# A two-model transformer kernel on one core: residue-order copies on GpSimd, maxima spread by transposes, and the cross attention rebuilt

## The chip, the cores and the metric

One core of a Trainium2 chip runs the whole program. The metric is the device time of one execution in microseconds (us), as a median over runs. A profiled execution gives the rows that are quoted here. In them PE is TensorE, PEld its weight loads, DVE is VectorE, ACT is ScalarE, POOL is GpSimd and SP is SyncE, whose queue issues all DMAs.

## The reference

A sequence of 512 tokens with 1024 channels passes through two blocks of two layers each, all in float32. The first block's layers have a dilated-window attention, a stick-breaking attention, gates and a convolutional feed-forward part. The second block's layers have a mixer (convolution and pooling in the first, mLSTM and latent attention in the second), a cross attention over 256 memory tokens, and a SwiGLU part.

```python
# first block, mixer A: query t attends keys t - j*dilation; three groups of heads
DSW_GROUPS = ((128, 1), (512, 4), (2048, 16))
def to_sub(a):
    a = a.reshape(B, L, dilation, H, hd).transpose(0, 2, 3, 1, 4)
...
# second block, in each layer after the mixer
def memory_cross_attention(h, mem_n, wq, wkv, wo):
    q = (h @ wq).reshape(B, S, XA_HEADS, XA_HEAD_DIM)          # 4 heads of 128
    k, v = jnp.split(mem_n @ wkv, 2, axis=-1)                   # 256 memory tokens
    ...
    s = jnp.einsum('bshd,bmhd->bhsm', q, k) * (XA_HEAD_DIM ** -0.5)
    p = jax.nn.softmax(s, axis=-1)
    return jnp.einsum('bhsm,bmhd->bshd', p, v).reshape(B, S, XA_WIDTH) @ wo

x = x + mix
mem_n = rmsnorm_2(mem, mem_norm_g[layer])
x = x + memory_cross_attention(rmsnorm_2(x, norm_xattn_g[layer]), mem_n, ...)
x = x + swiglu(rmsnorm_2(x, norm_ffn_g[layer]), ...)
```

## The kernel before

**Layout.** The activations `x` lie in SBUF with channels on partitions: 8 tiles (`KT`) of 128 channels by 512 tokens. Every projection is computed in three products of split operands: a value is split into a high part in fp32r and the remainder, `h_hi` and `h_lo` for activations, `w_hi` and `w_lo` for weights, and `product` (lines 607 to 609) issues high by high, high by low and low by high for each tile of the contraction. An operand that isn't split (scores, sums, values of an attention) goes through TensorE as plain float32; such a matmul leaves two records in the trace. A transpose against the identity leaves one.

**The weight stream.** The weights come in numbered chunks, in the order of `chunk_starts`: `qk`, `v`, `gate`, `br`, `wo`, `up`, `down` and so on. SP loads a chunk into `stage`, which holds one chunk in two parts; the load of a part waits until VectorE has taken the remainder of the same part of the chunk before (`w_lo_done`). ScalarE writes `w_hi` (line 1108) as soon as the chunk two places ahead of it has been used by TensorE (`w_used`), and VectorE writes `w_lo` from `stage` and `w_hi` (line 1503). So `w_hi` and `w_lo` hold two chunks. TensorE starts a chunk when its `w_lo` is done and the result banks `M` of the chunk two places before have been read (`m_free`). Each engine's order of work is written out by hand; an instruction that waits holds up everything behind it on its engine.

**First block.** `qk0` and `qk1` are 8 chunks each. The 4 chunks of values `v` follow (`token_major`): here activations are the stationary operand and 256 columns of weights the moving one. For the first and last chunk a stationary tile is 128 tokens in a row. For the two chunks between (groups 1 and 2), `residue_tile` picks every fourth token out of `h_hi` and `h_lo`, since these groups are attended in residue order. Then `mixture_head` runs 4 times a layer: scores, a part of the gate projections (`gate_tile`), the spread of the row maxima over partitions (line 747, a plain float32 matmul of a broadcast column with the identity, 12 for a head), more gate projection, 15 transposes of the probabilities (line 756), values. GpSimd does nothing.

**Cross attention, per layer (`cross_attention`).** Ahead of it stands the mixer's output product of 4 chunks: `ev_out` in the first layer, whose h tiles of the next norm are made while it runs, and `od_out` in the second, where `held=True` puts all 8 pairs of them behind its last chunk. Then TensorE does: the first chunk of q (`xq`), tile by tile as `h_lo` comes (`first_tiles`); the spread of the norm (line 666); 16 transposes of the memory, which VectorE copies to `mem_t`; the second chunk of q; 4 chunks of memory keys and values (`xkv`), with squares, sums and a norm of their own for the memory (`MEMORY`); and `attend`, a loop over 4 heads: scores of the next head, 8 transposes of the probabilities (line 931), a copy back by ScalarE (line 1357), the product with the values (line 937), and the split of the result into `xo_hi` and `xo_lo`. A head uses the four banks `A` or the four banks `M`. When all 4 heads are done, 4 chunks of `xo` (256 KB a part instead of 512) give the output product, and the feed-forward part starts with `first_tiles` over `up`.

Of the kernel before, what the change touches and what calls it, by code (L numbers as in the profile page):

```python
# [73 lines left out]
for _l in range(DEPTH):  # L74
    NORMS += [(KT if _l else 0, KT)] + ([(3, 3), (2, 2)] if _l else []) + [(KT, KT)] * 3
NORMS += [(KT, 0)]
LAST_NORM = len(NORMS) - 1
MIX, XATTN, MEMORY, FFN = ([5, 9], [6, 12], [7, 13], [8, 14])
LATENT_Q, LATENT_KV = 10, 11
# [58 lines left out]
def chunk_starts():  # L138
# [6 lines left out]
    for l in range(DEPTH):  # L145
# [5 lines left out]
        sizes += [(f"xq{l}", 2), (f"xkv{l}", 4), (f"xo{l}", 4)]  # L151
# [9 lines left out]
def block_program(nc, dram, out):  # L161
# [12 lines left out]
    with ExitStack() as ctx:  # L174
# [64 lines left out]
        def lay(*items):  # L239
# [17 lines left out]
        mem_t, mem_hi, mem_lo, k_x, v_x, q_x, x_prob, x_turned, mem_tok = lay(  # L257
            (8, "mem_t", [KT, N_MEM], F32),
# [71 lines left out]
        mem_turned, mem_out = sem("mem_turned"), sem("mem_out")  # L330
# [14 lines left out]
        chain = sem("chain")  # L345
        branch_done, value_done, col_root, col_done = (
# [17 lines left out]
        def head_banks(h):  # L364
            return A if h % 2 == 0 else M

# [15 lines left out]
        def gain_at(n, k):  # L382

            if n == MIX[0]:
# [3 lines left out]
                           MEMORY[0]: ("mem_norm_g_2", 0), MEMORY[1]: ("mem_norm_g_2", KT),  # L388
# [34 lines left out]
        def columns_before(n):  # L423

            return sum(j < n for j in (*WITH_COLUMNS, *MEMORY))
# [9 lines left out]
        def _(sp):  # L435
# [93 lines left out]
            def cross_attention(l):  # L529
                for n in range(2):  # L530
                    load_tiles(start[f"xq{l}"][0] + n, by_tile(dram["xattn_wq_2"][l]), 2 * n)
# [4 lines left out]
                for n in range(2):  # L536
                    load_wide(c0 + 2 + n, w, 2 + n)
                for n in range(4):
# [49 lines left out]
            for n in range(4):  # L588
                load_tiles(start["od_out"][0] + n, by_tile(dram["od_w_out_2"][0]), 2 * n)
                if n == 2:  # L590
# [10 lines left out]
        def _(pe):  # L601
# [38 lines left out]
            def token_major(c, s, hi, lo, k, tiles, pick=None):  # L640

                chunk_in(c)
                for t in range(tiles):
                    def tokens(n):
                        if pick is None:
                            return hi[:, n, t * P:(t + 1) * P], lo[:, n, t * P:(t + 1) * P]
                        return pick(hi[:, n, :], t), pick(lo[:, n, :], t)
# [8 lines left out]
            def norm(n, tokens=S):  # L656

                pe.wait_ge(square_added, additions(n + 1))
                if n in WITH_COLUMNS or n in MEMORY:
# [67 lines left out]
            def mixture_head(l, h):  # L727
# [115 lines left out]
            for l in range(DEPTH):  # L843
# [4 lines left out]
                for g in range(GROUPS):  # L848
                    def residue_tile(t, n, g=g):

# [1359 lines left out]
```

## Time and profile before

| | |
|---|---|
| median of 3 runs | 3119.66 us (3118.12 to 3121.15) |
| the profiled execution | 3118.83 us; its span, first to last instruction, 3116.7 us |
| instructions in it | 35330 |
| TensorE busy | 2946.1 us, 95% |
| VectorE, ScalarE, GpSimd busy | 1615.0, 1122.1 and 0.2 us |
| mean granted TensorE clock | 0.971 |
| HBM read | 247.86 MB, 80 GB/s over the span |

The profile page gives the busy time of each engine, the granted clock in 40 slices, the chain of work that ended last, and the costliest groups of instructions. Other views of the same trace give stretches (busy time, clock), waits (who waited for whom), the chain in order of time, and the instructions in order of time. Matmuls overlap in the pipeline, so their durations can't be added up; the distance between starts is what one costs in a run of them.

### The profile page before, as it was taken

How to read it: one execution, taken by the hardware profiler on the slowest of the kernel's cores; microseconds unless marked ns; L12 is line 12 of the kernel's file. 1: busy time of each engine (PE TensorE's matmuls, PEld its weight loads, DVE VectorE, ACT ScalarE, POOL GpSimd, SP SyncE). 2: the span in 40 equal slices, each digit the busy share in tenths (PEclk: the TensorE clock that was granted, in tenths of full speed). 3: DMA queues.
4: the chain of work that ended last, by engine and by line, in shares of the span. 5: the costliest groups of instructions: out<-in, count | busy, mean ns of one | idle time of the engine just before them, and what ended most of it. 6: DMA issues, size and time to landing. Idle time of an engine off the chain costs nothing.

```text
span 3116.7 us, 35330 instructions
## 1 busy us (share of the span) xinstructions
PE 2946.1 (95%) x13434; PEld 2398.0 (77%) x13434; DVE 1615.0 (52%) x2249; ACT 1122.1 (36%) x1544; POOL 0.2 (0%) x4
## 2 busy tenths in 40 slices
PE   5999989999999998999999989999996879899998
PEld 4898778888889877888888768888883547688886
DVE  3347656545534765644676554435443555454344
ACT  2116535324312653432442443223333243343222
POOL 0000000000000000000000000000000000000000
PEclk9999999999999999999999989999997889999999
DMA  3311123332331112333243223332320202133322
GB/s 116 95 41 55 55 81 94 90 100 87 101 95 41 55 54 81 101 91 105 83 123 95 88 62 100 87 108 82 108 74 4 58 21 68 57 106 94 108 84 78
DMA packets 465250, 251.37 MB, mean 81 GB/s; under 512 B 14982, under 2 KB 461279, under 8 KB 465023
## 3 DMA queue, kind: packets, MB, share of 16 engines
q1 hardware_dynamic: 465151, 250.00, 27.6%
q8 instruction: 69, 1.13, 0.1%
q14 instruction: 30, 0.25, 0.0%
HBM read 247.86 MB, written 2.10 MB: 80 GB/s over the span
## 4 chain that ended last, share of the span: by engine, by line
PE 88%; DVE 5%; ACT 3%; DMA 1%; issue 1%; SPq 0%; DVEq 0%; ACTq 0%
PE M L607 24%; PE M L609 24%; PE M L608 24%; PE M L682 2%; PE M L683 2%; PE M L684 2%; DVE w_lo L1503 1%; PE A L803 1%; PE A L739 1%; PE A L771 1%; PE A L937 1%; PE M L937 1%; PE A L747 1%; ACT w_hi L1108 1%; PE A L815 1%
## 5 line engine op out<-in xcount | busy, mean ns | idle before, releaser
L607 PE MATMUL M<-h_hi,w_hi 128*128 128x512 f32 (+1 forms) x2272 | 894.5, 394 | 1.7 <-DVE h_lo L1937 1.7
L609 PE MATMUL M<-h_hi,w_lo 128*128 128x512 f32 (+1 forms) x2272 | 886.2, 390 | 0.0
L608 PE MATMUL M<-h_lo,w_hi 128*128 128x512 f32 (+1 forms) x2272 | 886.1, 390 | 0.0
L1108 ACT ACTIVATE w_hi<-stage 128x1024 fp32r<-128x1024 f32 (+4 forms) x524 | 508.9, 1013 | 840.0 <-PE M L609 754.8
L1503 DVE TENSOR_TENSOR w_lo<-stage,w_hi 128x1024 fp32r<-128x1024 f32 (+4 forms) x524 | 595.6, 1174 | 133.9 <-ACT w_hi L1108 132.7
L607 PEld LDWEIGHTS M<-h_hi,w_hi 128*128 128x128 f32 (+1 forms) x2272 | 427.5, 188 | 94.7 <-issue 5.8
L608 PEld LDWEIGHTS M<-h_lo,w_hi 128*128 128x128 f32 (+1 forms) x2272 | 427.5, 188 | 90.7 <-issue 2.6
L609 PEld LDWEIGHTS M<-h_hi,w_lo 128*128 128x128 f32 (+1 forms) x2272 | 427.2, 188 | 90.2
L607 PE MATMUL M<-hid_hi,w_hi 128*128 128x512 f32 x704 | 274.6, 390 | 6.9 <-DVE hid_lo L1623 6.9
L608 PE MATMUL M<-hid_lo,w_hi 128*128 128x512 f32 x704 | 274.0, 389 | 0.0
L609 PE MATMUL M<-hid_hi,w_lo 128*128 128x512 f32 x704 | 273.9, 389 | 0.0
L1603 DVE TENSOR_TENSOR normed<-M,rstd 128x512 f32<-128x512 f32 x88 | 60.9, 692 | 313.7 <-PE M L609 282.0
L607 PEld LDWEIGHTS M<-hid_hi,w_hi 128*128 128x128 f32 x704 | 132.1, 188 | 36.7 <-DVE hid_lo L1623 9.5
L609 PEld LDWEIGHTS M<-hid_hi,w_lo 128*128 128x128 f32 x704 | 132.1, 188 | 27.6
L608 PEld LDWEIGHTS M<-hid_lo,w_hi 128*128 128x128 f32 x704 | 132.1, 188 | 27.3
L1579 DVE TENSOR_TENSOR x<-x,M 128x512 f32 x72 | 47.3, 684 | 142.7 <-PE M L609 133.3
L1224 ACT ACTIVATE hid_hi<-hid 128x512 f32 x88 | 55.6, 632 | 181.5 <-DVE hid L1621 181.5
L1630 DVE TENSOR_TENSOR x<-x,M 128x512 f32 (+1 forms) x40 | 27.5, 688 | 166.2 <-PE M L609 166.2
L1221 ACT ACTIVATE acted<-normed 128x512 f32<-128x512 f32 x44 | 27.8, 632 | 223.9 <-DVE normed L1603 223.9
L608 PE MATMUL M<-w_lo,h_hi 128*128 128x256 f32 x320 | 105.0, 328 | 0.0
L609 PE MATMUL M<-w_hi,h_lo 128*128 128x256 f32 x320 | 105.0, 328 | 0.0
L607 PE MATMUL M<-w_hi,h_hi 128*128 128x256 f32 x320 | 105.0, 328 | 0.0
(374 smaller groups left out, 3405.6 us busy)
## 6 DMA issues: line engine op xcount, KB each, us to landing
stage<-in_w_up SPq DMA_DIRECT2D x88, 512.0 KB, 4.4
stage<-in_ffn_w_gate_up SPq DMA_DIRECT2D x88, 512.0 KB, 4.2
stage<-in_w_in SPq DMA_DIRECT2D x80, 512.0 KB, 4.3
stage<-in_w_down SPq DMA_DIRECT2D x32, 384.0 KB, 3.7
stage<-in_ffn_w_down SPq DMA_DIRECT2D x32, 384.0 KB, 3.7
stage<-in_od_w_in SPq DMA_DIRECT2D x23, 512.0 KB, 4.0
stage<-in_w_down SPq DMA_DIRECT2D x32, 320.0 KB, 3.5
stage<-in_ffn_w_down SPq DMA_DIRECT2D x32, 320.0 KB, 3.5
```

Source lines behind the costliest of these rows:

```text
L607: pe.matmul(bank, a_hi, b_hi, start=(n == 0), stop=False)
L608: pe.matmul(bank, a_hi, b_lo, start=False, stop=False)
L609: last = pe.matmul(bank, a_lo, b_hi, start=False, stop=(n == k - 1))
L682: pe.matmul(bank, a_hi, b_hi, start=(j == 0), stop=False)
L683: pe.matmul(bank, a_hi, b_lo, start=False, stop=False)
L684: last = pe.matmul(bank, a_lo, b_hi, start=False, stop=(j == KT - 1))
L937: last = pe.matmul(bank[0][rows_, first_q[kt]:], values(h, kt), turned_[:, h % 2, turned_at[kt]:turned_at[kt] + S - first_q[kt]], start=(k ...
L1108: act.activation(w_hi[:, s, part * HALF:part * HALF + n], stage[:, part, 0:n], ACT.Copy)\
L1224: act.activation(hid_hi[:, i * 2 + s, :], hid[:, s, :], ACT.Copy).then_inc(hid_hi_done, 1)
L1503: dve.tensor_tensor(w_lo[:, s, part * HALF:part * HALF + n], stage[:, part, 0:n], w_hi[:, s, part * HALF:part * HALF + n].bitcast(F32), AL ...
L1579: added = dve.tensor_tensor(x[:, k + m, :], x[:, k + m, :], M[2 * s + m][:, :], ALU.add)
L1603: dve.tensor_tensor(branch_in[:, s, :], M[2 * s][:, :], rstd[:, :], ALU.mult)\
```

## The change

There are three edits.

1. **Residue-order copies.** GpSimd gets a program of its own: in each layer of the first block, as soon as the first `qk` chunk has been used, it copies `h_hi` and `h_lo` tile by tile into `hp_hi` and `hp_lo` with the tokens in residue order (16 copies of 128 by 512 a layer). The value chunks of groups 1 and 2 take their stationary tiles from these copies, each 128 tokens in a row, after a wait for all 16.
2. **Spread of the maxima.** The 12 matmuls of line 747 become 12 transposes.
3. **Cross attention.** The memory is prepared beside the mixer's output product: transposes into pairs of tiles in the banks `A` behind its first chunk, `mem_hi` and `mem_lo` made straight from the banks, squares by ScalarE from the token-major memory with the sum taken by the same instruction, and a spread by two transposes behind the second chunk. `mem_t`, the sums on VectorE and the norm `MEMORY` are gone. The order of chunks is `xkv`, `xq`, `xo` instead of `xq`, `xkv`, `xo`. A head takes two banks instead of four, two score tiles in each, so four heads are in flight in pairs. The second q chunk is cut in two products with the scores of heads 0 and 1 between, and the output product in parts (`part(n, k)`: chunk n, head k), which run between the transposes and values of heads 2 and 3. Loops over `od_out` and `xo` are unrolled. In the second layer the memory is loaded one chunk earlier.

```diff
@@ GpSimd
+        @block.gpsimd
+        def _(pool):
+            for l in range(DEPTH):
+                pool.wait_ge(w_used, start[f"qk{l}"][0] + 3)
+                for k in range(KT):
+                    pool.wait_ge(h_lo_done, split_norm(2 * l) + k + 1)
+                    pool.tensor_copy(as_residue(hp_hi[:, k, :], 1), by_residue(h_hi[:, k, :], 1)).then_inc(perm_done, 1)
+                    pool.tensor_copy(as_residue(hp_lo[:, k, :], 1), by_residue(h_lo[:, k, :], 1)).then_inc(perm_done, 1)
@@ TensorE, values
-                for g in range(GROUPS):
...
-                    token_major(c0 + g, g % 2, h_hi, h_lo, KT, TT, residue_tile)
+                token_major(c0, 0, h_hi, h_lo, KT, TT)
+                pe.wait_ge(perm_done, (l + 1) * 2 * KT)
+                for g in (1, 2):
+                    token_major(c0 + g, g % 2, hp_hi, hp_lo, KT, TT)
@@ TensorE, maxima
-                        last = pe.matmul(A[g][:, b * P:(b + 1) * P],
-                                         row_max[:, at + b:at + b + 1].broadcast_to([P, P]), ident,
-                                         start=True, stop=True)
+                        last = pe.transpose(A[g][:, b * P:(b + 1) * P],
+                                            row_max[:, at + b:at + b + 1].broadcast_to([P, P]), ident)
@@ chunk order, banks
-        sizes += [(f"xq{l}", 2), (f"xkv{l}", 4), (f"xo{l}", 4)]
+        sizes += [(f"xkv{l}", 4), (f"xq{l}", 2), (f"xo{l}", 4)]
+        cross_banks = (A[0:2], A[2:4], M[0:2], M[2:4])
+        xo_banks = (A[1::2], A[0::2], M[0:2], M[2:4])
@@ TensorE, cross attention
+            def memory_beside(l, n):
+                if n == 0:
...
+                        for t in range(N_MEM // P):
+                            last = pe.transpose(memory_tile(k)[:, t * P:(t + 1) * P], mem_tok[:, t, k * P:(k + 1) * P],
+                                                ident)
...
+                if n == 1:
+                    pe.wait_ge(mem_lo_done, KT * (l + 1))
+                    pe.wait_ge(mem_col, l + 1)
+                    for t in range(N_MEM // P):
+                        last = pe.transpose(A[0][:, t * P:(t + 1) * P], side_col[:, t:t + 1].broadcast_to([P, P]), ident)
...
             def cross_attention(l):
+                for n in range(2):
+                    two_tiles(c0 + n, n, memory, KT, n=N_MEM)
+                pe.wait_ge(mem_row, l + 1)
                 norm(XATTN[l])
                 for n in range(2):
                     token_major(c0 + 2 + n, n, mem_hi, mem_lo, KT, N_MEM // P)
+                c0 = start[f"xq{l}"][0]
+                pe.wait_ge(h_lo_done, split_norm(XATTN[l]) + KT)
+                two_tiles(c0, 0, normal, KT)
...
+                product(M[2][:, :], weight(1, 0), normal, KT)
+                pe.wait_ge(m_free, c0 + 3)
+                score(0)
+                score(1)
+                product(M[3][:, :], weight(1, 1), normal, KT).then_inc(w_used, 1)
+                turn(0)
+                turn(1)
+                pe.wait_ge(m_free, c0 + 4)
+                score(2)
+                score(3)
+                value(0)
+                value(1)
+                turn(2)
+                pe.wait_ge(w_lo_done, o0 * 2 + 2)
+                part(0, 0)
+                part(0, 1)
+                turn(3)
+                pe.wait_ge(w_lo_done, o0 * 2 + 4)
+                part(1, 0)
+                part(1, 1)
+                value(2)
+                value(3)
+                for n in range(2):
+                    part(n, 2)
+                    part(n, 3)
+                for n in range(2, 4):
+                    pe.wait_ge(w_lo_done, (o0 + n) * 2 + 2)
+                    for k in range(4):
+                        part(n, k)
@@ ScalarE, cross attention (VectorE: maxima and normalise in the same pairs, attended_lo)
+                split_after(c0, 0)
+                split_after(c0 + 1, 1)
+                norm_rows(XATTN[l])
+                split_after(c0 + 2, 0)
+                split_after(c0 + 3, 1)
...
+                exps(0)
+                exps(1)
+                back(0)
+                back(1)
                 split_after(c0 + 1, 1)
+                exps(2)
+                exps(3)
+                attended_hi(0)
+                attended_hi(1)
+                back(2)
+                back(3)
+                attended_hi(2)
+                attended_hi(3)
```

## Rows read from the trace of the kernel before

**Rows 1.** The profile page: busy time, granted clock, chain by engine.

```profile
PE 2946.1 (95%) x13434; PEld 2398.0 (77%) x13434; DVE 1615.0 (52%) x2249; ACT 1122.1 (36%) x1544; POOL 0.2 (0%) x4
...
PEclk9999999999999999999999989999997889999999
...
PE 88%; DVE 5%; ACT 3%; DMA 1%; issue 1%; SPq 0%; DVEq 0%; ACTq 0%
```

**Rows 2.** Stretches: value chunks; stretch and length, busy time (instructions) by engine, clock.

```profile
132.00:143.80 11.80, 11.80 (x99) 11.72 (x98) 3.56 (x4) 2.01 (x2) 0.00 (x0) 1.00 0.30 90
143.80:166.20 22.40, 22.40 (x98) 22.40 (x97) 3.93 (x6) 2.01 (x2) 0.00 (x0) 1.00 0.16 47
...
920.50:942.80 22.30, 22.30 (x98) 22.30 (x97) 3.92 (x6) 2.01 (x2) 0.00 (x0) 1.00 0.16 48
```

**Rows 3.** One line of VectorE (1811): durations ns min/median/max, first and last start.

```profile
L1811 DVE TENSOR_TENSOR qk_a<-M,rstd x24: 680/1078/1098, 57.7 to 888.4; 128x512 f32<-128x512 f32 x24
L1811 DVE TENSOR_TENSOR qk_b<-M,rstd x8: 680/686/692, 121.6 to 909.8; 128x512 f32<-128x512 f32 x8
```

**Rows 4.** The chain in order of time, one head: start us, us, what.

```profile
232.26 2.68 PE A L747 x24
240.42 1.64 PE A L756 x15
```

**Rows 5.** Stretches: cross attention, first layer, then second; columns as in rows 2.

```profile
1752.70:1777.00 24.30, 24.30 (x199) 23.86 (x198) 12.13 (x16) 8.54 (x12) 0.00 (x0) 1.00 0.41 127
...
1777.00:1817.60 40.60, 26.54 (x82) 15.07 (x81) 16.40 (x49) 15.39 (x46) 0.00 (x0) 0.75 0.05 16
...
sum 125.30, PE 110.82 PEld 87.35 DVE 71.76 ACT 54.76 POOL 0.00; mean PE 27.70 PEld 21.84 DVE 17.94 ACT 13.69 POOL 0.00
...
2614.50:2633.00 18.50, 12.67 (x49) 10.36 (x50) 10.15 (x14) 7.95 (x12) 0.00 (x0) 0.82 0.20 57
...
2671.60:2710.40 38.80, 24.12 (x80) 13.69 (x81) 16.25 (x49) 15.36 (x46) 0.00 (x0) 0.87 0.05 15
2710.40:2732.50 22.10, 22.04 (x96) 17.94 (x96) 15.20 (x21) 11.34 (x16) 0.00 (x0) 1.00 0.25 72
2732.50:2744.40 11.90, 11.13 (x49) 9.16 (x50) 9.33 (x13) 6.11 (x9) 0.00 (x0) 1.00 0.60 176
sum 129.90, PE 108.33 PEld 85.87 DVE 75.74 ACT 58.44 POOL 0.00; mean PE 21.67 PEld 17.17 DVE 15.15 ACT 11.69 POOL 0.00
```

**Rows 6.** Waits of TensorE, second layer's cross attention: us in total, times, longest.

```profile
PE M L682 <- DVE h_lo L1557: 5.8, 1, 5.8
PE A L931 <- DVE x_prob L1929: 3.9, 2, 3.3
```

**Rows 7.** The chain in order of time, first layer's attention: start us, us, what.

```profile
1778.01 2.01 PE A L966 x8
...
1780.04 1.43 DVE soft_max L1915 x4
...
1781.69 1.94 ACT x_prob L1348 x8
...
1783.87 1.15 DVE x_prob L1929 x4
...
1788.21 3.78 PE A L937 x4
...
1796.93 2.00 PE M L937 x4
...
1801.59 1.11 PE A L931 x8
```

**Rows 8.** VectorE in order of time, around the memory's chunks and behind `od_out`.

```profile
1761.86 2.36 DVE L1503 TENSOR_TENSOR w_lo<-stage,w_hi 128x1024 fp32r<-128x1024 f32 x2 [0.58 <-ACT w_hi L1108]
...
1769.74 1.23 DVE L1503 TENSOR_TENSOR w_lo<-stage,w_hi 128x1024 fp32r<-128x1024 f32 x1 [0.82 <-ACT w_hi L1108]
...
2619.44 5.38 DVE L1557 SCALAR_TENSOR_TENSOR h_lo<-x,vec,h_hi 128x512 fp32r<-128x512 f32 x8
```

More of the change, by code:

```diff
@@ L901, in _ @@
                 feed_forward(l, 2 * l + 1)
-            def looped_tiles(name, rhs, k):
-                c0, n = start[name]
-                with pe.Fori(0, n // 2) as i:
-                    for s in range(2):
-                        two_tiles(i * 2 + (c0 + s), s, rhs, k)
             def attend(kind, scores, values):
@@ new lines, in value @@
+                def value(h):
+                    pe.wait_ge(at_back, n0 + h + 1)
+                    for kt in range(N_MEM // P):
+                        last = pe.matmul(cross_banks[h][0][:, :], v_x[:, kt, h * P:(h + 1) * P],
+                                         x_turned[:, h % 2, kt * S:(kt + 1) * S],
+                                         start=(kt == 0), stop=(kt == N_MEM // P - 1))
+                    last.then_inc(at_pv, 1)
+                o0 = start[f"xo{l}"][0]
+                attended = operand(xo_hi, xo_lo)
@@ new lines, in part @@
+                def part(n, k):
+                    pe.wait_ge(at_out, n0 + k + 1)
+                    for m in range(2):
+                        last = product(xo_banks[n][m][:, :], weight(n % 2, m), attended, 4, k, k + 1)
+                    if k == 3:
+                        last.then_inc(w_used, 1)
+                chunk_in(c0 + 1)
+                product(M[2][:, :], weight(1, 0), normal, KT)
+                pe.wait_ge(m_free, c0 + 3)
+                score(0)
+                score(1)
@@ L1087, in _ @@
             pe.wait_ge(at_out, AT0["mla"] + MLA_HEADS)
-            looped_tiles("od_out", normal, KT)
+            for n in range(4):
+                two_tiles(start["od_out"][0] + n, n % 2, normal, KT)
+                memory_beside(1, n)
             cross_attention(1)
@@ L1491, in _ @@
             attend("mla")
-            splits_and_squares("od_out", XATTN[1], held=True)
+            splits_and_squares("od_out", XATTN[1], held=True, beside=1)
             cross_attention(1)
@@ L1587, in chunk @@
                             gained_lo(n_split, k + m)
-                with dve.Fori(0, n // 2) as i:
-                    for s in range(2):
-                        chunk(i * 2 + (c0 + s), s, i * (2 * per_chunk) + s * per_chunk)
+                if banks or beside is not None:
+                    for j in range(n):
+                        chunk(c0 + j, j % 2, j * per_chunk, banks[j] if banks else None)
+                        if j == 0 and beside is not None:
+                            memory_lo(beside)
+                else:
+                    with dve.Fori(0, n // 2) as i:
+                        for s in range(2):
+                            chunk(i * 2 + (c0 + s), s, i * (2 * per_chunk) + s * per_chunk)
                 for k in range(KT if held else 0):
@@ new lines, in attended_lo @@
+                def attended_lo(h):
+                    dve.wait_ge(at_hi, n0 + h + 1)
+                    dve.tensor_tensor(xo_lo[:, h, :], cross_banks[h][0][:, :], xo_hi[:, h, :].bitcast(F32), ALU.subtract)\
+                       .then_inc(at_out, 1)
+                maxima(0)
+                maxima(1)
+                normalise(0)
+                normalise(1)
+                dve.wait_ge(w_used, c0 + 4)
+                for m in range(2):
+                    last = dve.tensor_tensor(q_x[:, 2 + m, :], M[2 + m][:, :], rstd[:, :], ALU.mult)
```

209 lines of the change are left out of this document (130 added, 79 removed).

## The prediction

> **What bounds the kernel now.** I read the page first. TensorE is busy 95% of the span, the chain that ended last lies on it for 88%, and its clock is full in nearly every slice [rows 1]. So time comes back only where TensorE's own work shrinks, where it stands idle, or where its clock is low; work saved on another engine counts only if TensorE waited for it. Next I cut the stretches that the change touches out of the trace, to see which of the three each one is. The value chunks are pure work without idle time [rows 2]. The cross attention is the opposite: in the attention of the first layer TensorE is busy for 26.5 of 40.6 us at a mean clock of 0.75, in the second for 24.1 of 38.8 us at 0.87 [rows 5]. The waits name whom it waits for there [rows 6], and the chain in order of time shows one head as a loop through three engines [rows 7]. All sums below are made against the profiled execution (3118.8 us; span 3116.7), which is 0.8 us under the median of the runs.
>
> **Edit 1, residue-order copies.** A value chunk is 96 matmuls of 256 columns. The chunk with plain tiles takes 11.5 us (its stretch of 11.8 us has 99 records), the two with every fourth token 22.4 us each; all four of these, two in each layer, are 22.2 to 22.4 [rows 2]. In both kinds the weight loads fill the stretch as fully as the matmuls do, at full clock, with the same number of instructions: the load of a strided tile takes twice the time. The new tiles lie in a row, so the four chunks should take 11.5 us: 4 x (22.3 - 11.5) = 43.2 us less. Weights still come in time, since the plain value chunk holds this pace now and VectorE and ScalarE are busy for only 3.6 and 2.0 us of it [rows 2].
>
> The copies on GpSimd have no row. They start when the first `qk` chunk is used, at about 53 us, and must end at 143.8 us, where the second value chunk begins [rows 2]; the second layer has as much. 16 copies in 90 us hide as long as one takes under 5.6 us. Bound below: nothing. Bound above: VectorE takes 0.69 us for a plain 128x512 operation and 1.08 us with the residue order in it [rows 3]; even five times that is 5.4 us. I take 1 to 2 us, nearest to that row, hidden behind seven `qk` chunks: cost nothing. The cover lost, each us over 5.6 costs 16 us a layer.
>
> What speaks against GpSimd as the place is the Trainium skill, page "SBUF — State Buffer", section "SBUF: two separate sides": GpSimd and VectorE share a pair of ports, and a VectorE operation with two SBUF inputs, which the remainder of line 1503 is, waits out a whole GpSimd copy that began first. By a price on the page "GPSIMD Engine Reference", section 3.1 (about 0.77 us for 512 elements), that would be an estimate of 1.5 us a chunk; no row here shows GpSimd at work. From rows alone: line 1503 runs twice a chunk, and VectorE has about 7 us of a chunk free, so copies under 3.5 us can't make it late.
>
> **Edit 2, spread of the maxima.** 12 float32 matmuls leave 24 records and take 2.68 us; 15 transposes take 1.64 us, 0.109 each [rows 4]. 12 transposes take 1.31 us. ScalarE and VectorE have their part of a head done before TensorE gets to the next transposes, with more than a us to spare, so the gain stays: 8 heads x 1.37 = 11.0 us.
>
> **Edit 3, cross attention.** The stretch from the mixer's last product to the end of the first `up` chunk is 125.3 us in the first layer and 129.9 us in the second [rows 5]. I rebuild it from TensorE's work at full clock:
> - 16 transposes of the memory and 2 of the spread, 18 x 0.109 [rows 4]: 2.0.
> - Four `xkv` chunks: the stretch of 24.3 us holds them and 0.6 of the old memory norm [rows 5]: 23.7. The norm of x stays: 0.9.
> - `xo` with 96 matmuls of 512 columns: 22.0 [rows 5]. The two `xq` chunks have as many and no wait at their head, where the first matmul takes longer: 21.8.
> - Attention: 8 records of scores 2.0, 8 transposes 1.1, 4 records of values 2.0 [rows 7], each with about 0.2 of pipeline that overlaps when the next follows at once: 4.55 a head, 18.2 in all.
> - First `up` chunk: 11.1 [rows 5].
>
> Sum 99.7 us. Before, the rest was idle time and low clock: the value product of head 0 takes 3.78 us where that of head 1 takes 2.00 [rows 7], behind a wait for `x_prob` (3.3 us the longest [rows 6] in the other layer).
>
> Now what the new order leaves uncovered. Per pair of heads, scores end, then maxima 1.4, exponentials 1.9, normalising 1.15 a head [rows 7]: about 7 us until the second head's probabilities are ready. For heads 0 and 1 a q product of 5.4 us stands in front, and since head 0 starts while head 1's scores run, the transposes find both ready within some tenths. For heads 2 and 3 the values of 0 and 1 (3.7 us) cover head 2, and the parts of `xo` cover head 3. What is late is `xo_lo` of head 0, which stands on VectorE behind the normalising of head 2 and the remainder of an `xo` chunk, and on ScalarE behind the exponentials of 3: I count 0.7 us. The third `xo` chunk's weights can be split only when the first chunk's last part is done; 1.3 us of adds and 1.3 of remainders on VectorE just fit behind the two parts of chunk 1 (2.7 us). The first `up` chunk waits for its load, which waits for the split of the last `xo` chunk: 0.8 us. With 0.5 for sums I have rounded: 2.0 us of waits a layer.
>
> The four short `xkv` chunks in a row are now behind a long one. The single `stage` makes a cycle of load, high part, remainder: 1764.2 to 1771.0, 6.8 us [rows 8], against 5.9 of TensorE. In the first layer the reserve from the mixer's chunks and the 0.9 us norm cover it. In the second, VectorE still does the eight `h_lo` operations behind the last mixer chunk, 5.4 us [rows 8], before it can read out keys and split `xkv` chunk 2, which is then 0.8 us late, and each of the next two 0.8 more: 2.5 us. In turn TensorE no longer stands in front of them: before, it waited 5.8 us for `h_lo` [rows 6] and ran on at a low clock (12.7 of 18.5 us busy at 0.82 [rows 5]); now memory work fills that place.
>
> The memory's preparation moves beside the mixer's chunk 2. There VectorE gets eight operations of 0.4 us, ScalarE eight and two squares of 1 us: about 3 and 6 us beside chunks of 10.9 us in which they have 4.8 and 5 to 6.6 free. ScalarE comes up to 1 us late for the next weights, which are wanted 10 us later: nothing. The earlier load of the memory waits on SP for the last rope product, and the `od_out` load queued behind it isn't needed until two chunks on: nothing.
>
> First layer: 125.3 - 99.7 - 2.0 = 23.6 us. Second: 129.9 - 99.7 - 2.0 - 2.5 = 25.7 us. Together 49.3 us.
>
> **Sum.** 43.2 + 11.0 + 49.3 = 103.5 us. The profiled execution becomes 3015.3 us, the median 3016 us.
>
> **Rivals.**
> - *The pairs don't cover.* Every handover in the new order has a cover of a few us only, and a stall of 3 us costs twice, since the clock then runs at its lower level (1.2 instead of 2.4 GHz) for the next product [rows 6, 7]. For it: TensorE's order is fixed, with up to three engines in one link. Against it: by my count no link misses by over 1 us. If half of what idle time and clock cost in the two attentions (40.6 + 38.8 - 36.4 = 43.0 us) comes back, 21.5 us, it is 3038 us.
> - *The strided read isn't the cause.* If the doubled chunk came from the order of accumulation or the banks, edit 1 gives nothing: 3059 us. Against: the weight loads themselves fill the doubled stretch.
> - *GpSimd is late (the side of slower).* If a copy takes 8.9 us, TensorE stands before the second value chunk for 3.3 x 16 = 52 us a layer and the whole gain is gone; at 10 us it is 3157 us. Copies that long would also hold up line 1503. Nothing in the trace is near this: it is eight times the slowest VectorE row of this shape [rows 3].
> - *Waits a little longer than counted* in the weight cycle or at `xo_lo`, 2 to 5 us a layer: 3020 to 3026, inside my range.
>
> **Chances.** Forecast with its small waits 0.80, pairs don't cover 0.14, strided read 0.02, GpSimd late 0.02, something unseen in between 0.02. No case but GpSimd late ends at or over the time before (a change under 0.2%, 6 us, could not be told from none). Faster 0.97, same 0.01, slower 0.02. Range: without any wait, 6.5 us less, and with a us for rounding, 3008; upwards nearly to the first rival's 3038, since its milder forms lie before that: 3036.
>
> **What would show it.** The windows of value chunks 2 and 3 at 11.5 us; GpSimd's 32 copies at 1 to 2 us and no wait of TensorE for them; line 747 with 96 records instead of 192; the attention and `xo` of a layer without waits over 1 us and with a clock of 1.00; waits for `w_lo` of under a us at `xkv` in the second layer and before `up` in both. Wrong it would be if TensorE waits for `x_prob` or `xo_lo` by 2 us and the clock falls behind it, or if copies reach 5.6 us.

## The result, and the profile after

| | before | after |
|---|---|---|
| median beside each other | 3120.40 us (3118.12 to 3121.30, 4 executions) | 3017.88 us (3013.72 to 3020.23, 4) |
| ratio to before | | 0.9672, 95% interval 0.9659 to 0.9684 |
| profiled execution, span | 3118.83, 3116.7 us | 3018.72, 3016.9 us |

The time fell by 102.5 us, 3.3%; the forecast was 3016 us. Taken again later, the same kernel had a median of 3023.41 us beside 3121.47 before, 98.1 us less. On the page of the kernel after, TensorE's busy time is 78.6 us lower, its busy share has stayed at 95% [rows 1], and GpSimd has 35.7 us of work. Busy time (share, instructions) by engine, the clock in 40 slices and the chain by engine:

```profile
PE 2867.5 (95%) x13330; PEld 2334.8 (77%) x13330; DVE 1615.4 (54%) x2199; ACT 1119.0 (37%) x1534; POOL 35.7 (1%) x36
...
PEclk9999999999999999999999999999997789999999
...
PE 88%; DVE 6%; ACT 3%; DMA 1%; issue 1%; SPq 0%; DVEq 0%; ACTq 0%
```

The first three of the first layer's value chunks after (columns as in [rows 2]):

```profile
135.34:146.85 11.51, 11.51 (x97) 11.51 (x96) 3.56 (x4) 2.01 (x2) 0.00 (x0) 1.00 0.32 93
146.85:158.45 11.60, 11.60 (x99) 11.60 (x98) 3.92 (x6) 2.01 (x2) 0.00 (x0) 1.00 0.30 90
158.45:170.05 11.60, 11.60 (x99) 11.60 (x98) 3.93 (x6) 2.01 (x2) 0.00 (x0) 1.00 0.33 92
```

The second and third cost what the first does now; the fourth takes 11.45 us. From the start of the first to the end of the fourth it is 46.2 us instead of 67.9, in the second layer 46.2 instead of 67.9: 43.5 us less in both. Line 747 is line 759 now, with half the records, which is what a transpose leaves (durations ns min/median/max, first and last start):

```profile
L759 PE MATMUL A<-const,row_max x96: 271/272/323, 190.7 to 1008.0; 128*128 128x128 f32 x96
```

The first layer's cross attention after (columns as in [rows 5]): the end of the output product, `xkv` and most of the q product; the rest of it, attention and the first two `xo` chunks; the other two with their waits; first `up` chunk.

```profile
1679.60:1728.00 48.40, 48.40 (x305) 43.84 (x304) 25.52 (x39) 18.16 (x31) 0.00 (x0) 1.00 0.38 109
1728.00:1758.60 30.60, 28.85 (x128) 20.88 (x127) 17.18 (x38) 16.06 (x40) 0.00 (x0) 1.00 0.09 24
1758.60:1771.50 12.90, 10.52 (x46) 8.04 (x44) 11.32 (x16) 7.82 (x11) 0.00 (x0) 1.00 0.42 122
1771.50:1782.60 11.10, 11.10 (x49) 9.07 (x50) 8.56 (x12) 5.35 (x8) 0.00 (x0) 1.00 0.59 174
```

Attention had a clock of 0.75 and a third of idle time before [rows 5]; now the clock is 1.00 throughout and idle time is short. What idle time is left, in the first and then in the second layer, is this (line 621 is the first matmul of a product, line 607 before; line 694 is the first `up` chunk; columns as in [rows 6]):

```profile
PE M L694 <- DVE w_lo L1638: 1.9, 1, 1.9
PE M L621 <- DVE w_lo L1638: 1.4, 2, 0.9
PE A L621 <- DVE xo_lo L2129: 0.8, 1, 0.8
...
PE M L621 <- DVE w_lo L1638: 3.0, 4, 0.9
PE M L694 <- DVE w_lo L1638: 1.7, 1, 1.7
...
PE A L621 <- DVE xo_lo L2129: 0.8, 1, 0.8
PE M L621 <- issue: 0.6, 1, 0.6
```

**Where the 99.8 us of span went.** From the start of the program to the start of `ev_out`, 48.3 us: value chunks 43.5 and maxima 10.9 less, but the start up to the value chunks 3.0 more and one wait 3.1 more. The 3.0 us are mostly clock: the first tiles ran at 0.80 (before 1.00) and the first 10 us behind them at 0.86 (before 1.00). The kernel with paced copies, below, shows the same (0.85), so it isn't the copies' doing; what it is, is open. From there to the end of the first `up` chunk, 22.0 us (168.8 to 146.8). From there to the start of `od_out`, where no edit lies, 5.7 us. From the start of `od_out` to the end of the second layer's first `up` chunk, 23.8 us (175.1 to 151.3). After that nothing (372.4 both).

**The wait that I had ruled out.** It stands in `qk1` of the second layer: TensorE waits 3.04 us for `w_lo`. VectorE in order of time has there

```profile
808.40 1.29 DVE L1960 TENSOR_TENSOR qk_a<-M,rstd 128x512 f32<-128x512 f32 x2 [8.19 <-ACT rstd L1280]
809.89 12.48 DVE L1638 TENSOR_TENSOR w_lo<-stage,w_hi 128x1024 fp32r<-128x1024 f32 x2 [0.21 <-ACT w_hi L1191]
```

and GpSimd

```profile
808.67 1.14 POOL L1181 CAST hp_lo<-h_lo 128x512 fp32r<-128x512 f32 x1
809.77 1.12 POOL L1180 CAST hp_hi<-h_hi 128x512 fp32r<-128x512 f32 x1
810.84 1.08 POOL L1181 CAST hp_lo<-h_lo 128x512 fp32r<-128x512 f32 x1
...
819.08 1.07 POOL L1181 CAST hp_lo<-h_lo 128x512 fp32r<-128x512 f32 x1
```

Two remainders that take 2.36 us elsewhere take 12.48. They end at 822.37, 2.2 us behind the last copy (820.15), which is the time that the pair takes alone: so both seem to have run only when the string of copies was over. In the first layer the same pair took 4.12 us and nobody waited.

### The profile page after: what moved, and what is told of

Read it like the earlier page. It is cut to its first block, busy times and chain, and to the rows that moved or that the text cites. A ratio compares the mean times of both kernels' runs of the same rounds, so it can differ in the third digit from the quotient of the medians.

```text
span 3016.9 us, 34891 instructions
## 1 busy us (share of the span) xinstructions
PE 2867.5 (95%) x13330; PEld 2334.8 (77%) x13330; DVE 1615.4 (54%) x2199; ACT 1119.0 (37%) x1534; POOL 35.7 (1%) x36
## 4 chain that ended last, share of the span: by engine, by line
PE 88%; DVE 6%; ACT 3%; DMA 1%; issue 1%; SPq 0%; DVEq 0%; ACTq 0%
PE M L621 24%; PE M L622 24%; PE M L623 24%; DVE w_lo L1638 2%; PE M L694 1%; PE M L695 1%; PE M L696 1%; PE A L814 1%; PE A L751 1%; PE A L782 1%; PE A L826 1%; PE A L1099 1%; ACT w_hi L1191 1%; PE A L795 0%; PE A L767 0%
## 5 line engine op out<-in xcount | busy, mean ns | idle before, releaser
L621 PE MATMUL M<-h_hi,w_hi 128*128 128x512 f32 (+1 forms) x2304 | 907.8, 394 | 5.0 <-DVE w_lo L1638 3.0
L622 PE MATMUL M<-h_lo,w_hi 128*128 128x512 f32 (+1 forms) x2304 | 899.1, 390 | 0.0
L623 PE MATMUL M<-h_hi,w_lo 128*128 128x512 f32 (+1 forms) x2304 | 898.8, 390 | 0.0
L1638 DVE TENSOR_TENSOR w_lo<-stage,w_hi 128x1024 fp32r<-128x1024 f32 (+4 forms) x524 | 608.6, 1199 | 147.5 <-ACT w_hi L1191 146.4
L621 PEld LDWEIGHTS M<-h_hi,w_hi 128*128 128x128 f32 (+1 forms) x2304 | 433.9, 188 | 100.4 <-issue 8.1
L623 PEld LDWEIGHTS M<-h_hi,w_lo 128*128 128x128 f32 (+1 forms) x2304 | 433.6, 188 | 91.0
L1779 DVE TENSOR_TENSOR x<-x,M 128x512 f32 (+1 forms) x40 | 27.5, 688 | 166.1 <-PE M L623 166.1
L1722 DVE TENSOR_TENSOR x<-x,M 128x512 f32 (+1 forms) x64 | 42.2, 685 | 126.7 <-PE M L623 117.5
L1772 DVE TENSOR_TENSOR hid_lo<-hid,hid_hi 128x512 f32 x88 | 61.0, 693 | 81.7 <-ACT hid_hi L1327 81.7
L1762 DVE SCALAR_TENSOR_TENSOR conv<-normed,vec,conv 128x511 f32<-128x511 f32 x88 | 66.1, 751 | 45.4 <-ACT conv L1316 39.0
L1316 ACT ACTIVATE conv<-normed,vec 128x512 f32<-128x512 f32 x44 | 35.9, 816 | 140.4 <-DVE normed L1752 140.3
```

The source lines that it names most:

```text
L621: pe.matmul(bank, a_hi, b_hi, start=(n == 0), stop=False)
L622: pe.matmul(bank, a_hi, b_lo, start=False, stop=False)
L623: last = pe.matmul(bank, a_lo, b_hi, start=False, stop=(n == k - 1))
L1316: act.activation(conv[:, s, :], branch_in[:, s, :], ACT.Identity, bias=col_at("conv_b", i * 2 + (l * FT + f0 + s)), scale=col_at(f"conv_w{ ...
L1638: dve.tensor_tensor(w_lo[:, s, part * HALF:part * HALF + n], stage[:, part, 0:n], w_hi[:, s, part * HALF:part * HALF + n].bitcast(F32), AL ...
L1722: added = dve.tensor_tensor(x[:, k + m, :], x[:, k + m, :], bank[:, :], ALU.add)
```

## The experiments

Each was timed over five rounds beside the kernel before. "Profiled" is its one profiled execution. The three values in the column "before" stand for three sittings, each on another chip; across sittings the ratios are the fairer measure, since the kernel before itself moved by 2.4 us.

| kernel | median (range), us | before, us | ratio, 95% interval | profiled |
|---|---|---|---|---|
| edit 1 alone | 3087.98 (3076.64 to 3095.97) | 3119.08 | 0.9900, 0.9882 to 0.9918 | 3079.59 |
| edit 1 alone, again | 3081.97 (3073.76 to 3087.39) | 3121.47 | 0.9873, 0.9853 to 0.9893 | 3073.76 |
| plain tiles, no copies | 3074.61 (3071.72 to 3077.45) | 3119.08 | 0.9856, 0.9843 to 0.9869 | 3075.48 |
| edit 1 alone, paced copies | 3072.87 (3072.16 to 3075.53) | 3121.47 | 0.9844, 0.9827 to 0.9861 | 3072.87 |
| edit 2 alone | 3108.47 (3103.77 to 3113.01) | 3119.08 | 0.9965, 0.9952 to 0.9979 | 3109.42 |
| edit 3 alone | 3070.71 (3068.11 to 3076.04) | 3119.08 | 0.9848, 0.9836 to 0.9861 | 3068.11 |
| after, again | 3023.41 (3017.83 to 3028.49) | 3121.47 | 0.9686, 0.9666 to 0.9705 | 3019.99 |
| after, paced copies | 3011.15 (3008.95 to 3019.35) | 3121.47 | 0.9648, 0.9628 to 0.9668 | 3012.42 |
| paced, sizes | 3009.94 (3008.97 to 3017.22) | 3119.83 | 0.9655, 0.9642 to 0.9668 | 3009.45 |
| paced, late h | 3011.16 (3008.02 to 3016.92) | 3119.83 | 0.9653, 0.9640 to 0.9666 | 3011.16 |
| paced, no cover | 3028.42 (3027.36 to 3032.83) | 3119.83 | 0.9710, 0.9697 to 0.9723 | 3027.88 |
| all three | 3009.18 (3008.86 to 3012.75) | 3119.83 | 0.9648, 0.9634 to 0.9661 | 3011.70 |

**The edits one by one.** First edit 1 (its diff is the GpSimd and values part of the change):

> The kernel before with edit 1 alone (copies in residue order on GpSimd, value chunks of groups 1 and 2 read from them). My step: the four strided chunks fall from 22.3 to 11.5 us, 43.2 us less in all, and the copies cost nothing: 3077 us. Second theory, from the trace of the kernel after: the copies run as one string of some 17 us and hold VectorE's remainder of a weight chunk until the string ends, so TensorE waits once for it, 3.0 us in the second layer and nothing in the first: about 40 us less, 3080 us. What tells them apart is the wait for the weight remainder in the qk chunks, 0 or 3 us, and the duration of that remainder (2.35 us as in other chunks, or over 4). Rival (the strided read isn't the cause): no change, 3120 us.

The value chunks without any copies; this kernel leaves out the residue order of groups 1 and 2:

```diff
-                        r = by_residue(t, g)
-                        return r[:, n, :]
+                        return t[:, n * P:(n + 1) * P]
```

> The kernel before, but the value chunks of groups 1 and 2 take 128 tokens in a row straight from h_hi and h_lo; no copies, GpSimd does nothing. It leaves out the residue order of these two groups' values, so they are attended in the wrong order of tokens. It prices the strided read by itself. My step: 43.2 us less, 3077 us, without any wait for the weight remainder in the qk chunks. Second theory (the string of copies costs 3 us): this kernel is 3 us faster than the one with edit 1 alone. If copies cost nothing, the two are equal. Rival (the strided read isn't the cause): no change, 3120 us.

The strided read is worth 44.5 us, as in my step (43.2). But edit 1 alone gives only 31.1 and scatters over 19 us. The copies cost 13.4 us in the median, not 0 and not 3: both theories missed the price. The mechanism of the second is there, in the other layer: a pair of remainders of 12.42 us in the first layer (4.05 in the second), and one wait of TensorE for `w_lo`, 4.6 us. The wait isn't all that it costs: from the spread of the norm to the first value chunk TensorE took 83.4 us there and 77.1 without copies, 6.3 us more.

> The kernel before with edit 2 alone (the 12 spreads of the row maxima of a head as transposes instead of matmuls). My step: 8 heads x 1.37 us = 11.0 us less, 3109 us. If a hand-over of VectorE or ScalarE fills part of what is freed, 5 to 9 us less and a wait of TensorE before the transposes of the probabilities in its place; if a float32 matmul and a transpose cost the same and something else gave the gain after, 0.

10.6 us less, as expected; the profile has 96 records of the spread.

> The kernel before with edit 3 alone (cross attention rebuilt: memory beside the mixer's product, heads in pairs, q and output products cut). My step: 23.6 + 25.7 = 49.3 us less, 3070 us. By the trace of the kernel after the two stages give 22.0 and 23.8 = 45.8 us: 3074 us. If the stage gains more only because the edits before it changed the clock or the state in which it is entered, it is well off both. The stretch between the first cross attention and the od_out chunks was 5.7 us shorter after than before without an edit in it: if edit 3 caused that (through the order of what is loaded or the clock), it is here too and the whole is 51 us less, 3069 us; if it came from edit 1 or 2, it isn't here.

48.4 us less in the median, near my step. The profiled execution is 50.7 us shorter, which fits the 45.8 us and the branch with the untouched stretch: most of that stretch's gain is here too (80.2 us instead of 85.0, see below). The three parts, without GpSimd's share, add up to 44.5 + 10.6 + 48.4 = 103.5 us.

**The string of copies.** The kernel after was taken again unchanged, and with GpSimd's copies spread over the `qk` chunks:

```diff
             for l in range(DEPTH):
-                pool.wait_ge(w_used, start[f"qk{l}"][0] + 3)
                 for k in range(KT):
-                    pool.wait_ge(h_lo_done, split_norm(2 * l) + k + 1)
+                    pool.wait_ge(w_lo_done, (start[f"qk{l}"][0] + k + 2) * 2 + 2)
+                    pool.wait_ge(h_lo_done, split_norm(2 * l) + KT)
```

> The kernel after, unchanged, as the measure for the runs beside it: 3017.9 us. First theory (VectorE's remainder of a weight chunk is held while the string of GpSimd copies runs, and how many of the 16 copies hold it differs from run to run): the executions scatter over 10 us or more, and the profile shows a remainder of 3 to 12 us in at least one of the two layers. Rival (the 3.0 us wait of the second layer belongs to the order of work): the same wait in the same place again.

> The kernel after with GpSimd's copies paced: a pair of copies starts when VectorE has finished the remainder of the weight chunk two places on, so the pairs fall in VectorE's free time, one a chunk. Theory (the string holds the remainder): every remainder of the qk chunks at 1.2 us a part, no wait of TensorE for w_lo there, 3 us less than the kernel after in a profiled run and 3 to 10 in the median, with less scatter; 3008 to 3015 us. Rival (the wait comes from a late load or from ScalarE, and the long remainder is only how the wait looks): the 3 us wait stays and the time is that of the kernel after.

The median falls by 12.3 us, the profiled execution by 7.6. Every remainder of the `qk` chunks takes its normal time and no wait for them is left, so the rival is out. The scatter stays 10 us with either, with the copies paced because of one execution at 3019 (the other four: 3009 to 3012). In the unchanged kernel both layers were held this time, VectorE in order of time:

```profile
59.17 12.42 DVE L1638 TENSOR_TENSOR w_lo<-stage,w_hi 128x1024 fp32r<-128x1024 f32 x2 [0.22 <-ACT w_hi L1191]
...
814.47 12.53 DVE L1638 TENSOR_TENSOR w_lo<-stage,w_hi 128x1024 fp32r<-128x1024 f32 x2 [0.21 <-ACT w_hi L1191]
```

and TensorE's waits for them in the two stretches are

```profile
PE M L621 <- DVE w_lo L1638: 4.6, 1, 4.6
...
PE M L621 <- DVE w_lo L1638: 3.1, 1, 3.1
```

together 7.7 us. That this is also the difference between the two profiled executions is a coincidence, for in the first layer TensorE went on at a low clock behind the wait (columns as in [rows 2]):

```profile
71.73:82.00 10.27, 10.27 (x33) 8.19 (x34) 4.29 (x4) 2.11 (x2) 0.00 (x0) 0.70 0.70 202
```

From the spread of the norm to the first value chunk it took 84.9 us, against 78.6 with paced copies and 77.1 with plain tiles and no copies: the wait of 4.6 us cost 6.2 to 7.7. In the second layer the wait of 3.1 us brought no drop, and the stretch is 2.8 us longer than with paced copies. Together that is at least 9.0 us for two held pairs, nearer to the 12.3 of the median. SP, too, is late: it can load the next weights only when `stage` is free (70.48 us), so ScalarE's next high part starts at 74.35 us, 14.3 us after the last had ended. With paced copies GpSimd works in VectorE's gaps (GpSimd, then VectorE):

```profile
63.67 1.08 POOL L1180 CAST hp_hi<-h_hi 128x512 fp32r<-128x512 f32 x1 [63.22 <-DVE w_lo L1638]
64.69 1.08 POOL L1181 CAST hp_lo<-h_lo 128x512 fp32r<-128x512 f32 x1
74.26 1.08 POOL L1180 CAST hp_hi<-h_hi 128x512 fp32r<-128x512 f32 x1 [8.48 <-DVE w_lo L1638]
```

```profile
61.25 2.36 DVE L1638 TENSOR_TENSOR w_lo<-stage,w_hi 128x1024 fp32r<-128x1024 f32 x2 [0.22 <-ACT w_hi L1191]
69.83 2.09 DVE L1960 TENSOR_TENSOR qk_a<-M,rstd 128x512 f32<-128x512 f32 x2 [6.22 <-PE M L623]
71.82 2.38 DVE L1638 TENSOR_TENSOR w_lo<-stage,w_hi 128x1024 fp32r<-128x1024 f32 x2
```

The same on the kernel before with edit 1 alone, unchanged and paced:

> The kernel before with edit 1 alone, again: its six executions lay between 3077 and 3096 us, those of the kernel without copies between 3072 and 3077. Theory (chance decides how long the string of copies holds VectorE's remainder): again 3077 to 3096 with a scatter of over 10 us, median 3080 to 3090, and in the profile a remainder held for 3 to 15 us and a wait of TensorE for w_lo of 0 to 15 us that makes up the difference to 3075. Rival (the scatter was the state of that chip): now within 5 us, near 3077.

> The kernel before with edit 1 alone, the copies paced as described for the kernel after: one pair for each qk chunk, each behind VectorE's remainder of the chunk two places on. Theory (only the string costs): 3075 us with a scatter of 5 us, as the kernel without copies, 13 us less than edit 1 alone. Rival (GpSimd's copies cost through the memory ports wherever they stand, for instance by slowing ScalarE or TensorE's reads): 3080 to 3088 us as edit 1 alone.

Paced it is 3072.87 us with a scatter of 3 us, 9.1 us under the unpaced kernel beside it, and by the ratios (0.9844 and 0.9856) the same as the kernel without copies; unpaced again a scatter of 14. So copies in the gaps cost nothing that these runs can tell from none. This time the profiled execution was a mild one, and shows the other way in which the two engines share. VectorE, then GpSimd:

```profile
60.18 4.01 DVE L1511 TENSOR_TENSOR w_lo<-stage,w_hi 128x1024 fp32r<-128x1024 f32 x2 [0.22 <-ACT w_hi L1116]
70.24 3.25 DVE L1511 TENSOR_TENSOR w_lo<-stage,w_hi 128x1024 fp32r<-128x1024 f32 x2
```

```profile
59.95 1.12 POOL L1105 CAST hp_hi<-h_hi 128x512 fp32r<-128x512 f32 x1
61.01 2.09 POOL L1106 CAST hp_lo<-h_lo 128x512 fp32r<-128x512 f32 x1
63.04 2.09 POOL L1105 CAST hp_hi<-h_hi 128x512 fp32r<-128x512 f32 x1
65.07 1.09 POOL L1106 CAST hp_lo<-h_lo 128x512 fp32r<-128x512 f32 x1
```

Here VectorE got in after one copy, twice, and two copies took 2.09 instead of 1.1 us. So in these profiles a pair of remainders either alternates with copies (4.0 us, no wait behind it) or stands until the last of them (12.4 us). Four profiles with unpaced copies have eight layers, and in four of these the pair was held to the end: both of the kernel after again, the second of the kernel after, and the first with edit 1 alone.

**The waits left in the cross attention.** Three kernels with paced copies, each with one more edit, and one with all. Sizes:

```diff
-                    split_hi(c + 2, s)
+                    split_hi(c + 2, s, size[c + 2] if isinstance(c, int) and n == 4 else HALF)
...
-                    split_lo(c + 2, s)
+                    split_lo(c + 2, s, size[c + 2] if isinstance(c, int) else HALF)
```

> The kernel after with paced copies (3011 us), and the high parts and remainders of output chunks 2 and 3 of the cross attention made over the 512 columns that these chunks have, not over 1024. Theory (the waits of 0.9, 0.5 and 1.7 to 1.9 us before the xo chunks 2 and 3 and the first up chunk come from splits twice as long as I had counted, 2.35 instead of 1.3 us on VectorE): the three waits fall from 3.0 us a layer to under 1.5, 3 to 4 us less in all, 3007 to 3008 us. Rival (they come from the load of the chunk, which is late by itself): the waits stay within 0.3 us, 3011 us.

The cause is right, the price half of it. VectorE's remainder behind the first `xo` chunk, with paced copies alone and then with the sizes:

```profile
1751.41 2.36 DVE L1638 TENSOR_TENSOR w_lo<-stage,w_hi 128x1024 fp32r<-128x1024 f32 x2
```

```profile
1749.56 1.28 DVE L1638 TENSOR_TENSOR w_lo<-stage,w_hi 128x512 fp32r<-128x512 f32 x2
```

The two waits inside `xo` (1.2 us a layer) are gone, that before `up` only falls from 1.7 to 1.5 in the first and 1.9 to 1.6 us in the second layer, and in the latter 0.4 us of waiting for `h_lo` comes up. That is 2.5 us less waiting, and 3.0 us in the profiled executions; the medians, 1.2 us apart and from two sittings, lie inside each other's ranges, and the ratios (0.9655 and 0.9648) show no gain.

Late h tiles: the held pairs moved from behind the mixer's last chunk to behind the first two `xkv` chunks, on both engines:

```diff
-                for k in range(KT if held else 0):
+                for k in range(KT if held and beside is None else 0):
...
+                for k in range(KT if l else 0):
+                    gained_lo(XATTN[l], k)
```

> The kernel after with paced copies (3011 us), and in the second layer the eight pairs of h tiles of the cross attention's norm, which stand on VectorE and ScalarE behind the last mixer chunk, made behind the read-out of the first two xkv chunks. Theory (these eight h_lo operations, 5.4 us, are what makes the remainders of xkv chunks 2 and 3 late, 1.9 us of waits): the waits at xkv go, 2 us less, 3009 us. Rival (the waits are the cycle of the one stage, load, high part, remainder, longer than TensorE's chunk): they stay at 0.9 us each, 3011 us. If the h tiles come too late for the q chunk, a wait for h_lo of up to 5 us stands there instead.

The 1.9 us of waits for `w_lo` at `xkv` went. But ahead of the q product TensorE now stands 1.4 us where it stood 0.5. The profile puts this down to "issue", but VectorE in order of time shows the releaser:

```profile
2550.90 5.39 DVE L1694 SCALAR_TENSOR_TENSOR h_lo<-x,vec,h_hi 128x512 fp32r<-128x512 f32 x8
...
2556.99 2.35 DVE L1640 TENSOR_TENSOR w_lo<-stage,w_hi 128x1024 fp32r<-128x1024 f32 x2
```

The remainders of the first q chunk now stand behind the eight `h_lo` operations and end at 2559.34 us; TensorE starts 0.1 us later. So the h tiles did make the remainders late, and moved they make the next ones late. Net 1.1 us less waiting in this layer, no difference in the median (3011.16 against 3011.15). Neither theory's number held.

All three edits, and the remainder of the next chunk ahead of the adds for the first two output chunks:

```diff
+                    first = pair is not None and c < c0 + 2
+                    if first:
+                        split_lo(c + 2, s, size[c + 2])
```

> The kernel after with all three: paced copies, splits over the chunk's own columns (and for output chunks 0 and 1 the next remainder ahead of the adds), and the late h tiles of the second layer. If the three causes are separate, the waits add up: 3011 less 3 to 4 less 2 = 3005 to 3006 us, some 12 us under the kernel after. If the single stage limits the stretch, one of them only moves the wait to the next chunk: 3008 us or more.

3009.18 us: no better than the sizes alone, and 2.0 us under paced copies in another sitting (both have the ratio 0.9648), so no gain is shown. The waits of both cross attentions are 9.9 us with paced copies, 7.4 with the sizes, 8.7 with late h tiles and 7.4 with all, where the wait before `up` is 2.2 us in each layer. In the first layer that wait is followed by a low clock (0.85), and the first `up` chunk takes 12.6 us instead of 11.4 with the sizes alone. So the causes do not add up; what is saved moves on to `up`, which fits the single stage as the limit, though no run varied the stage itself. Against the kernel after, unchanged, it is the pacing that counts.

**Is the cover needed?** The second q product goes ahead of the scores:

```diff
                 chunk_in(c0 + 1)
                 product(M[2][:, :], weight(1, 0), normal, KT)
+                product(M[3][:, :], weight(1, 1), normal, KT).then_inc(w_used, 1)
                 pe.wait_ge(m_free, c0 + 3)
                 score(0)
                 score(1)
-                product(M[3][:, :], weight(1, 1), normal, KT).then_inc(w_used, 1)
```

> The kernel after with paced copies (3011 us), and the second product of the q chunk, 5.4 us, put ahead of the scores of heads 0 and 1 instead of between these scores and the transposes of their probabilities. The work is the same. Theory (a head needs 4 to 7 us through VectorE and ScalarE, so this product hides it, and it is the cut that gives the gain): TensorE waits 4 to 6 us for x_prob in each layer, and the clock behind the wait falls for some us at 1.2 GHz: 5.4 to 9 us a layer, 3022 to 3029 us. Rival (the gain is from four heads in flight and the longer order would hold anyhow): under 2 us a layer, 3011 to 3015 us. If a stall costs no clock, 8 to 11 us in all.

17.3 us slower than with the cover by the medians of two sittings, and 17.3 to 19.2 slower than the three kernels of its own sitting that have the cover: the theory holds. In both layers the stretch from the start of the q product to the start of `up` grew by 6.0 us (65.9 to 71.9, and 66.2 to 72.2). In the first layer 3.9 us of it are waits for `x_prob` (in the second 3.2), as the chain in order of time has them (head 0's maxima, the exponentials of both heads, and head 1's normalising):

```profile
1724.07 1.30 DVE soft_max L2108 x2
...
1725.60 3.76 ACT x_prob L1491 x16
...
1729.60 1.15 DVE x_prob L2123 x4
...
1730.79 1.72 PE A L986 x8
1732.51 2.79 PE M L977 x8
```

and the other 2.1 us lie in the same transposes and scores at a lower clock, behind the wait. The stretches of that kernel: scores and wait, transposes and next scores.

```profile
1722.14:1728.97 6.83, 3.62 (x17) 2.85 (x15) 4.24 (x11) 3.37 (x15) 0.00 (x0) 1.00 0.00 0
1728.97:1736.85 7.88, 7.15 (x32) 6.19 (x33) 3.97 (x10) 3.58 (x8) 0.00 (x0) 0.78 0.00 0
```

The two layers make 12 us. The remaining 5 us of the median are not in the attention; in the profiled execution 4.7 lie in the stretch of the next paragraph, which this edit doesn't touch either.

**A stretch that no edit touches.** From the first small matmul of the mLSTM to its `cq` product TensorE does the same in every kernel, in short bursts between waits. Its row in the kernel before, with plain tiles and no copies, and after:

```profile
2347.90:2432.90 85.00, 57.23 (x124) 28.52 (x125) 23.85 (x39) 28.94 (x61) 0.00 (x0) 0.70 0.00 0
```

```profile
2301.80:2389.20 87.40, 59.54 (x125) 29.46 (x125) 23.87 (x39) 28.97 (x61) 0.00 (x0) 0.68 0.00 0
```

```profile
2277.60:2357.30 79.70, 50.49 (x125) 26.30 (x125) 23.86 (x39) 29.00 (x61) 0.00 (x0) 0.76 0.00 0
```

VectorE and ScalarE have the same work to 0.1 us; only TensorE's clock differs (0.68 to 0.76) and with it its busy time. Over the six profiles without edit 3 the stretch takes 84.2 to 87.4 us in five and 80.2 in one; over the eight with it 79.7 to 81.8 in seven and 84.8 in one (no cover). So 5.3 of the 5.7 us between the kernels before and after lie here. It leans towards edit 3, with an exception on each side. Why is open; no run was aimed at it. It may also be why the kernel after with paced copies gains 110.3 us (3121.47 to 3011.15) where the three parts sum to 103.5; that isn't shown either.

## Why the prediction was right

The forecast was 3016 us, with a chance of 0.8 for it and its small waits, and the time 3017.88. Point by point:

- *Edit 1, value chunks: 43.2 us.* 43.5 in the trace, 44.5 and 48.6 in the medians of the two kernels that have the plain tiles without held remainders. The rival that the strided read isn't the cause is out.
- *Edit 1, copies cost nothing.* This step failed. Their size was right (1.07 to 1.14 us, in my range of 1 to 2; beside a remainder up to 2.12), and for the value chunks they were never late. But "copies under 3.5 us can't make line 1503 late" reckoned with one copy at a time. Ten in a row held it together, and TensorE lost 3.0 us in the profiled execution, at least 9.0 in another (7.7 of waits and the low clock behind one of them), and in the median the copies cost 9.1 to 13.4 us (12.3 in the kernel after). For executions above the profiled ones no trace shows where the rest was lost. By the Trainium skill, page "SBUF — State Buffer", section "SBUF: two separate sides", which I weighed for this step, VectorE waits while GpSimd holds the ports; the trace agrees for a single copy (60.18 to 61.07, then it gets in). I had drawn from it that an instruction waits out one copy at most, and the rows with 12.4 us show otherwise.
- *Edit 2: 11.0 us.* 10.9 in the trace, 10.6 alone.
- *Edit 3: 23.6 and 25.7 us.* 22.0 and 23.8 in the trace. TensorE's work was right; the terms that were too small are waits: 4.1 us in the first layer instead of 2.0, and 6.0 instead of 4.5 in the second. The third `xo` chunk's split does not "just fit": I took 1.3 us for the remainders, and they run over 1024 columns for a chunk of 512 and take 2.36. That costs 0.9 and 0.5 us inside `xo`. Before `up` it was 1.9 and 1.7 us, not 0.8, and most of that is not the sizes. `xo_lo` was 0.8 (0.7 counted), `xkv` 1.8 and 0.6 before the q product (2.5 counted).
- *The rival that the pairs don't cover*: no wait for `x_prob` is left. The kernel without the cover shows that its mechanism is real: 3.9 us of stall cost 6.0. "Costs twice" was too much as a rule: the held remainder's 4.6 us cost 6.2 to 7.7, and its 3.0 us in the second layer 2.8, without a drop of the clock.
- *Balance.* The sum for the profiled execution was 3.4 us too low. In its favour there was a stretch that no edit touches (5.7 us), against it the shortfall of edit 3 (3.5), the held remainder (3.1) and a later start (3.0). With 12 us for the copies in the median and 5.7 from a stretch that I had not looked at, part of the closeness is luck: with paced copies the gain is 110.3 us, 6.8 over my sum, so a cost that I had put at nothing and a gain that I had not counted nearly cancelled. The second measurement, 98.1 us, was less close.

## What to carry to other kernels

Work moved to an engine that "has time" is to be placed in the gaps of the engine with which it shares a port, not started as soon as its input is there: pacing the same 32 copies by a semaphore of VectorE's work gave 12 us in the kernel after and 9 in that with edit 1 alone. When a product is cut to hide another engine's turn, count what that turn takes (here 1.3 + 3.8 + 1.2 us for two heads) and put at least that much between; a stall of 3.9 us cost 6.0, since the clock fell behind it. When something is said to have cost a wait, compare the whole stretch and not only the wait. Compare the stretches that an edit does not touch before crediting the whole difference to it.

## What the runs showed of the hardware

- A string of GpSimd copies back to back can keep a VectorE instruction with two SBUF inputs out for the whole string: 10 copies of 1.08 us, 12.4 us for a pair of remainders that takes 2.36, in four of eight layers. In the other four it got in after one copy (4.0 us). What decides between the two isn't shown.
- In the mild case the copy that runs beside VectorE takes 2.09 us instead of 1.08. VectorE's scaling out of PSUM (line 1960, 1.29 us for two) was not held by the copies that ran beside it.
- A stationary tile of every fourth token (values of 4 bytes) doubled the weight load, and with it a product of 256 columns whose loads fill the whole stretch: 22.4 against 11.5 us a chunk.
- A stall of TensorE can cost more than its length, but need not: 4.6 us of waiting cost 6.2 to 7.7 (granted clock 0.70 in the 10 us behind it, 0.85 in the kernel with edit 1 alone), 3.9 cost 6.0 (0.78), and 3.0 cost 2.8 with no drop. What decides isn't shown.
- In a stretch of short bursts the granted clock differs from kernel to kernel at the same work (0.68 to 0.76), which is 7.7 us on 80.
